# Twenty-six products that nobody reads, on TensorE around the slot table of a mixture-of-experts kernel

## The reference

```
g_logits = t @ rg_w + rg_b;  grp = argmax(g_logits)          # 4 groups
e_sel = (t @ re_w + re_b)[grp];  top_v, top_i = top_k(e_sel, 2)   # 2 of 8 in the group
top_w = softmax(top_v) * p_grp
hid = silu(t @ w_gate[e]) * (t @ w_up[e])                    # 1024 -> 256, per expert
y   = sum over the picked e of (hid * combine[e]) @ w_down[e] # 256 -> 1024
x   = layer_norm(ALPHA * x + gt2 * y, ln2_g, ln2_b)
```

## Time and profile before

| | us |
|---|---|
| timed runs (3) | 749.69, 756.36, 758.58; median 756.36 |
| profiled execution | 743.48 |
| its span, first to last instruction | 741.7 |
| TensorE busy, matmuls / weight loads | 615.8 / 407.4 |
| VectorE / ScalarE / GpSimd busy | 328.9 / 134.9 / 102.9 |
| mean granted clock | 0.897 |
| moved by DMA | 181.07 MB, 244 GB/s over the span |

### The profile page before, as it was taken

One profiled execution on the slowest core, in us unless ns is written; L12 is line 12 of the kernel. 1 busy time (PEld: TensorE's weight loads), 2 busy tenths in 40 slices (PEclk: granted clock), 3 DMA queues, 4 the chain that ended last, 5 costly groups with the idle time before them and its releaser, 6 DMA issues.

```text
span 741.7 us, 11297 instructions
## 1 busy us (share of the span) xinstructions
PE 615.8 (83%) x4698; PEld 407.4 (55%) x4698; DVE 328.9 (44%) x602; ACT 134.9 (18%) x356; POOL 102.9 (14%) x144
## 2 busy tenths in 40 slices
PE   3779999999998798999744999888788887788594
PEld 1549999888985564454433655444444444445241
DVE  2282442565533553375685244433333333343248
ACT  1442441244342053011120110000000000000100
POOL 3000000100001203000011133311222222232100
PEclk9569999999998797999955899998999999999897
DMA  8991311211008799601499599999999999996243
GB/s 287 344 258 60 66 59 57 72 57 58 26 32 256 233 368 279 187 30 43 169 384 337 192 392 407 407 408 405 405 408 407 408 405 400 403 406 271 87 178 117
DMA packets 90237, 181.07 MB, mean 244 GB/s; under 512 B 22164, under 2 KB 54780, under 8 KB 90180
## 3 DMA queue, kind: packets, MB, share of 16 engines
q1 hardware_dynamic: 79556, 163.39, 60.9%
q0 software_dynamic: 7936, 14.09, 5.7%
q10 hardware_dynamic: 2688, 2.77, 1.1%
HBM read 176.25 MB, written 14.45 MB: 257 GB/s over the span
## 4 chain that ended last, share of the span: by engine, by line
PE 47%; SPq 25%; DVE 11%; DMA 8%; issue 5%; ACT 4%; ACTq 0%; DVEq 0%; POOLq 0%
SPq L414 24%; PE bank L922 9%; PE bank L1139 8%; PE bank L974 7%; PE bank L1243 6%; DMA ring<-in_ada_w_dram 4%; PE bank L876 3%; PE bank L1261 3%; DMA ring<-in_moe_w_up_dram 3%; PE bank L1102 1%; PE bank L1106 1%; PE bank L1297 1%; PE bank L1025 1%; PE bank L1013 1%; DVE x_tok L1787 1%
## 5 line engine op out<-in xcount | busy, mean ns | idle before, releaser
L1243 PE MATMUL bank<-late_w,xT 128*64 128x256 f32 x672 | 89.7, 428 | 24.6 <-DMA late_w<-in_moe_w_up_dram 20.7
L1243 PEld LDWEIGHTS bank<-late_w,xT 128*64 128x64 f32 x672 | 55.7, 154 | 64.7 <-DMA late_w<-in_moe_w_up_dram 31.3
L1724 DVE COPY xT<-bank 128x512 f32<-128x512 f32 x36 | 24.7, 691 | 126.1 <-PE bank L1229 125.8
L1243 PE MATMUL bank<-ring,xT 128*64 128x256 f32 x480 | 62.8, 421 | 14.0 <-DMA ring<-in_moe_w_up_dram 12.2
L1243 PEld LDWEIGHTS bank<-ring,xT 128*64 128x64 f32 x480 | 38.5, 152 | 42.4 <-DMA ring<-in_moe_w_up_dram 20.5
L819 ACT ACTIVATE sgl<-bank 128x128 f32<-128x128 f32 x36 | 10.0, 278 | 249.6 <-PE bank L1243 249.5
L577 POOL DMA_INDIRECT xg<-h_scratch,srci x38 | 38.8, 1022 | 108.1 <-PE bank L1229 96.2
L584 POOL DMA_INDIRECT expert_rows<-ye,dsti x36 | 36.5, 1014 | 123.5 <-DVE ye L1743 123.5
L1740 DVE SCALAR_TENSOR_TENSOR S<-bank,modrt,S 128x512 f32<-128x512 f32 x36 | 27.0, 751 | 37.3 <-PE bank L1261 37.3
L974 PE MATMUL bank<-ring_r,h_high 128*128 128x256 f32 (+2 forms) x320 | 42.4, 283 | 0.0
L1261 PE MATMUL bank<-late_w,hT 128*64 128x512 f32 x168 | 40.7, 604 | 1.2 <-issue 1.2
(11 more groups left out here) (306 smaller groups left out, 898.9 us busy)
## 6 DMA issues: line engine op xcount, KB each, us to landing
ring<-in_ada_w_dram SPq DMA_DIRECT2D x22, 1024.0 KB, 9.3
late_w<-in_moe_w_gate_dram SPq DMA_DIRECT2D x21, 1024.0 KB, 16.3
late_w<-in_moe_w_up_dram SPq DMA_DIRECT2D x21, 1024.0 KB, 20.1
late_w<-in_moe_w_down_dram SPq DMA_DIRECT2D x21, 1024.0 KB, 20.2
ring<-in_moe_w_down_dram SPq DMA_DIRECT2D x15, 1024.0 KB, 20.0
ring<-in_moe_w_up_dram SPq DMA_DIRECT2D x15, 1024.0 KB, 19.9
ring<-in_moe_w_gate_dram SPq DMA_DIRECT2D x15, 1024.0 KB, 15.6
ring<-in_w_in_dram SPq DMA_DIRECT2D x7, 1024.0 KB, 5.9
```

Of the source, the lines that this page charges most:

```text
L1243: mm = pe.matmul(bank[2 + a][f * C:(f + 1) * C, 0:2 * P], x, w[:, kk, f, :, :], start=(kk == 0), stop=(kk == KD - 1))
L1724: dve.tensor_copy(xT[:, a, :, :], bank[a][:, :].rearrange("p (k n) -> p k n", k=4)).then_inc(xe_ev, 1)
```

## The change

A helper `keep_running(n)` issues n products of `ident` (stationary) with `ones` (moving) into bank 4, columns 0 to 127. Nothing reads the result, and no semaphore is raised. It is called twice on TensorE's stream: with 12 behind the product of the block starts (L1204) and ahead of the wait for `hot_ready`; and with 14 behind the waits for `tbl_ready` and `wsl_ready` and ahead of `turn_x(0, ...)`, whose first step is the wait for the gathered rows. Nothing else is moved or removed.

```diff
--- before.py
+++ after.py
@@ -1190,6 +1190,10 @@
             route(NT - 1)
 
 
+            def keep_running(n):
+                for _ in range(n):
+                    pe.matmul(bank[4][:, 0:P], ident[:, :], ones[:, :], start=True, stop=True)
+
             pe.wait_ge(oh_ready, 1)
             pe.wait_ge(pl, NSLOT)
             ranks = bank[0][:, 0:NT * E].rearrange("p (j e) -> p j e", j=NT)
@@ -1203,6 +1207,7 @@
             pe.wait_ge(extra_ready, 1)
             pe.matmul(bank[2][:, 0:E + 1], extra[:, 0:1].to_broadcast([E, P]), before[0:E, 0:E + 1],
                       start=True, stop=True).then_inc(pe_start, 1)
+            keep_running(12)
             pe.wait_ge(hot_ready, 1)
             for k in range(2):
                 for j in range(NT):
@@ -1264,6 +1269,7 @@
 
             pe.wait_ge(tbl_ready, 1)
             pe.wait_ge(wsl_ready, 2)
+            keep_running(14)
             turn_x(0, 16, None)
             for e in range(E + 1):
                 if e < E:
```

## The result

| | before | changed |
|---|---|---|
| median of 12 runs each, us | 756.95 (741.13 to 759.17) | 758.34 (750.97 to 761.94) |
| profiled execution, its span | 743.48, 741.7 | 761.67, 759.9 |
| mean granted clock in it | 0.897 | 0.888 |

The ratio is 1.0134 with the interval 1.0071 to 1.0197. It compares the fastest runs alone, and one run of before at 741.13 leaves only four of its twelve in that comparison, so it overstates the loss; the medians differ by 0.2%, the means (754.5 and 757.7) by 3.2 us. I take the change as some 3 us slower. What follows shows why from the profiles: these separate the stretches of one execution, which the times cannot.

What follows compares the result with a forecast made beforehand. The prediction took the weight stream as the bound, its start fixing its end. Gather 1.0, transposes 0.3 and first gate/up block 0.7 made 2.0 us: 756.36 - 2.0 = 754.4 us, range 745.4 to 759.5.

Steps and rivals of the forecast that it cites:

- What bounds: SyncE's weight stream: an earlier end of the first gate/up block moves the kernel's end equally, pass-through 1.
- The twelve: Unread products behind L1204: 4.5 to 5.4 us at the low clock, costing 0.1 us, clock up near L1211's start.
- The table: Slot table product L1211, 2.89 us before: 1.1 us saved at the higher clock, bounds 0.2 and 1.45.
- The gather: First gather on GpSimd: issued 1.0 us earlier (1.1 - 0.1), rows landing at about 405.3 instead of 406.3.
- The fourteen: Unread products before the wait for gathered rows: 2.7 us at full clock, too short to keep it up.
- The gate/up block: First gate/up block: clock falls again before it, 5.8 us against 6.48, 0.7 us saved.
- The turn: Four transposes of the gathered rows, 1.10 us before: 0.3 us saved.
- The local sum: Gather 1.0, transposes 0.3 and first gate/up block 0.7 us: 2.0 us earlier in all.
- Rival two: Unread products outlast the pauses and delay the turn: 2.5 us lost, 758.9 us; chance 0.16.
- The range: Whole kernel's measured time: 745.4 to 759.5 us, mostly the spread of the timed runs.

Runs made afterwards that it cites:

- wide: The changed kernel with its unread products up to 512 columns wide, 28 instructions instead of 104; median 755.02 us, 755.59 for before beside it, ratio 0.997.
- nested_keep: Kernel before with nested pair conditions and wide products: 12 columns' worth in the first pause, 22 in the second, 3 behind the transposes; median 747.30 us, ratio 0.999.
- after_152: The changed kernel with 76 more unread two-column products (152 instructions) ahead of L1196; median 755.62 us, 756.57 for before beside it, ratio 1.000.
- nested_wide: Kernel before with nested pair conditions (one taken branch instead of six) and the change's products in 28 wide instructions; median 752.22 us, ratio 0.991.
- nested_second: Kernel before with nested pair conditions and only the fourteen products of the second pause; median 749.25 us, 755.24 for before beside it, ratio 0.998.

## Why the prediction was wrong

**What bounds** held: the gain at the first gate/up block went through the whole weight stream (279.1 and 278.8 us).

**The twelve**: forecast 4.5 to 5.4 us and a cost of 0.1, measured 4.45 to 5.49 in eight profiles; the table was on time in six and 0.3 us late in two. They raised the clock by the table in all. **The table**: 1.1 us forecast, 1.12 measured. **The gather**: 1.0 us earlier forecast, 1.12 measured, and its rows came 0.17 us sooner after it.

**The fourteen**: 2.7 us forecast, 3.36 measured, 0.120 us for each of the 28. The row of L1086 (half the array's rows) was the wrong one for the full clock. The weight loads are not what makes the difference: in wide the same columns pass with 8 loads in place of 28 and still take 3.24 us. The longer time cost nothing, as the idle stretch behind it took it up.

**The gate/up block**: 5.8 us forecast with ends 5.36 and 6.59, measured 5.36 in both profiles of the changed kernel. The turn: 0.35 us saved, 0.3 forecast. The local sum was 2.0 us forecast and 2.8 measured. The argument that the clock falls again in that pause was right, and nested_keep shows what it costs: 5.36 less 3.67, 1.7 us. That the size fits is in part luck: where the clock rose late, in after_152 and nested_wide, the block took 5.75 and 5.87 us.

**The step that failed** is the sentence that nothing waits behind the 52 added matmuls but TensorE's own next instructions. I priced 104 instructions at the time that they run and not at the place that they push the later code to. The price was 6.1 us, at the skipped expert pairs 290 us later: one instruction fetch more, and a slow one. The view was at hand: the chain of waits before has 8.34 us of "issue" ahead of L1297 (shown with the result), more than the whole change could bring, and I passed over it as it was not in the changed stretch. With it the sum is -2.8 + 6.1 = +3.3 us, which is also the difference of the two totals (355.7 less 352.4), against 3.2 us between the means. That these agree so well is chance: the second pair of profiles differs by 6.1 us (355.7 less 349.6).

Rival two, with 758.9 us, came nearest to the measured 758.34 for a wrong reason: its delay exists (1.5 us in nested_second) but not in the changed kernel. **The range** held the median (its upper end adds up to 759.4, not 759.5). Its basis was thin in one respect: I took the profiled execution's distance from the median as unexplained, where the clock ahead of the change explains it.

## What to carry to other kernels

Instructions that do nothing still move everything behind them. Where a kernel has branches over long unrolled bodies, look in the chain of waits for "issue" at each, measure it again after any edit ahead of it, and nest conditions that fail together so that one is taken. Here that nesting was worth more (4.8 us of total) than the products of the change were with it (1.2 us). Unread products do raise TensorE's clock, but to hold it they must leave only a short pause ahead of the first product that profits: 1.4 us was short enough in nested_second, 3.9 us was not in the changed kernel. Wide ones move the same columns in a quarter of the instructions, and so shift the code less.

## What the runs showed of the hardware that I had not expected

- Six skips over unrolled blocks of about 180 matmuls and weight loads each cost TensorE 8.3 to 8.8 us or 14.3 to 14.5 us, by where the code lay; a shift of 256 instructions gave the first value again; one skip over them all cost 1.5 to 1.9 us, and in one of six kernels 2.6 us more one product later.
- Instruction packets of some 16 KB came 3.0 to 3.6 us apart during these skips, three in the short gaps (the first just ahead of them) and four in the long ones, the fourth 5.9 to 6.4 us behind the third.
- The same program ran its first 400 us with a spread of 15 us between executions (389.3 to 404.9 us to the block starts), and the granted clock from 100 to 150 us was 1.00 in the shorter and 0.80 in the longer.
- An f32 product of 128 rows, 128 stationary and 128 moving columns costs 0.240 us at the full clock in a row of its kind (3.36 us for 14). Fourteen that start at the low clock take 5.81 us, and at the full clock the same columns in products of up to 512 take 3.24 us.
- Twelve f32 products with the identity brought the clock up before they ended, in 4.5 to 5.5 us; 3.9 us of pause, transposes and copy let it fall again.
